# Differential attention: one combined pass over both halves, the first half's inverse applied when the output is stored, and a minimum of negated logits

## Chip, cores and metric

One core of a Trainium2 chip (trn2) runs the whole program, a chain of three transformer layers, in one launch. The metric is the device time of that launch in microseconds.

## The reference, cut to what matters

The changed stage is `diff_attention` of the second layer: 1024 tokens, 8 heads, query and key halves of 64, values of 128, in blocks of 128 queries.

```python
def diff_attention(q, k, v, lam, rel_table):
    ...
    def block(args):
        ...
        s = jnp.einsum("bqhcd,bkhcd->bhcqk", qi, k).astype(jnp.float32) * scale + bias[None, :, None]
        s = jnp.where(rel >= 0, s, -jnp.inf)
        p = jax.nn.softmax(s, axis=-1)
        w = p[:, :, 0] - lam * p[:, :, 1]
        return jnp.einsum("bhqk,bkhv->bqhv", w.astype(v.dtype), v)
```

Each head has two softmaxes, c = 0 and 1. With e the exponentials and z their sums, the weights are w = e0/z0 - lam e1/z1. The output of each head then goes through an RMS norm over its 128 values, a gain, and a gate.

## The kernel before

`diff_attend` (L2505) is one block of code on all engines, between barriers. The stages around it start after it and end before it. It walks through 8 heads, and in each through 8 blocks of 128 queries; block qb needs (qb + 1) x 128 keys, so every width from 128 to 1024 comes once a head. The first and the last head are written out, and the six between run in a hardware loop of two heads a turn. Every engine has its own fixed order of instructions, and semaphores connect them:

- TensorE, for each k: `logits` of block k + 2 (L2655; both halves, two matmuls for each 512 keys, into the one accumulator pS that a half has), `values` of block k - 1 (L2668, into one of two banks of pO), `turn` of block k (L2679, which transposes the weights W into pE). `logits` of block 0 of a head waits for GpSimd's split of that head's keys (`x_split`, L2657).
- VectorE, for each k: `bias` of block k + 1, `combine` of block k, `keep` of block k - 1; at k = 1 the `norm` of the head before, at k = 2 and 3 its `move_head`. `bias` (L2728) reads the logits from PSUM, adds the bias, scales, and keeps the row's maximum, for each half, and then negates both maxima (L2742). `combine` (L2744) takes the reciprocals of both sums (L2748), multiplies that of half 1 by the lambda factor (L2750; `lam` holds the negated factor), writes half 1 times it to W (L2753), and adds half 0 times its reciprocal (L2755). `keep` (L2758) copies the value product from PSUM to O (L2762).
- ScalarE, for each k: `exps` of block k + 1 (L2815: exponent with the negated maximum as bias, and the sum), `move` of block k (L2823, the transposed weights from PSUM to ET, L2827), `squares` of block k - 1 (L2829). At k = 1 comes the `root` of the head before (L2835), at k = 3 `round_head` of the next head (L2811, L2813).
- GpSimd, for each head: `gate` of the head before (L2620), `set_bias` of the next (L2601), `store`, and `subtract` of the next head (L2606), two long instructions at L2612 and L2615 that read and write SBUF and end with `x_split`.
- SyncE issues the loads of raw queries and keys and of values, a head ahead.

The lines that matter most:

```python
dve.tensor_scalar(v[:, :, 1:2], v[:, :, 0:1], -1.0, None, ALU.mult).then_inc(neg, 1)           # L2742
dve.tensor_scalar(W[:, qb % 2, 0:w], E[:, qb % 2, 1, 0:w], v[:, 1, 3:4], None, ALU.mult)        # L2753
dve.scalar_tensor_tensor(W[:, qb % 2, 0:w], E[:, qb % 2, 0, 0:w], v[:, 0, 3:4], W[:, qb % 2, 0:w],
                         ALU.mult, ALU.add).then_inc(comb, 1)                                   # L2755
dve.tensor_copy(O[:, s, qb, :], pO[:, qb % 2, 0:D_V]).then_inc(kept, 1)                         # L2762
```

Of the kernel before, what the change touches and what calls it, by code (L numbers as in the profile page):

```python
# [14 lines left out]
ACT = mybir.ActivationFunctionType  # L15
AX = mybir.AxisListType

P = 128
L = 1024
# [2485 lines left out]
def diff_attend(nc, tag, qkT, vg, skew, far, lam, subln, ident, yT):  # L2505
# [3 lines left out]
    with Place(nc, tag) as pl:  # L2509
# [9 lines left out]
        mx = pl.sb("mx", [P, 2, 2, 4])  # L2519
# [22 lines left out]
        neg = pl.sem("negated")  # L2542
        expd = pl.sem("exp_done")
        inv = pl.sem("weights_ready")
        half = pl.sem("second_half_weighted")
# [24 lines left out]
        with nc.Block() as block:  # L2570
# [150 lines left out]
            def _(dve):  # L2721
                dve.sem_inc(masked, 2)
                dve.sem_inc(comb, 2)
                dve.sem_inc(kept, 2)
# [3 lines left out]
                def bias(h, s, qb):  # L2728
                    w, m = (qb + 1) * P, h * TT + qb
                    v = mx[:, qb % 2, :, :]  # L2730
                    if qb == 0:
                        dve.wait_ge(b_in, h + 1)
                        dve.wait_ge(b_far, h + 1)
                    for a in range(2):
                        dve.wait_ge(dots, 2 * m + a + 1)
                        dve.wait_ge(expd, 2 * m + a + 1)
                        dve.sem_inc(passed, 1)
                        dve.tensor_tensor_reduce(S[:, qb % 2, a, 0:w], pS[:, a, :, :].rearrange("p a b -> p (a b)")[:, 0:w],  # L2738
                                                 B[:, s, L - w:L], D_QK ** -0.5, GONE, ALU.add, ALU.max,
                                                 v[:, a, 0:1]).then_inc(masked, 1)  # L2740
                    dve.wait_ge(masked, 2 * m + 4)
                    dve.tensor_scalar(v[:, :, 1:2], v[:, :, 0:1], -1.0, None, ALU.mult).then_inc(neg, 1)  # L2742

                def combine(h, qb):  # L2744
                    m, w = h * TT + qb, (qb + 1) * P
                    v = mx[:, qb % 2, :, :]
# [3 lines left out]
                    dve.tensor_scalar(v[:, 1, 3:4], v[:, 1, 3:4], lam[:, :], None, ALU.mult).then_inc(inv, 1)  # L2750
                    dve.wait_ge(inv, 2 * m + 2)
                    dve.wait_ge(turned, m + 1)
                    dve.tensor_scalar(W[:, qb % 2, 0:w], E[:, qb % 2, 1, 0:w], v[:, 1, 3:4], None, ALU.mult).then_inc(half, 1)  # L2753
                    dve.wait_ge(half, m + 1)
                    dve.scalar_tensor_tensor(W[:, qb % 2, 0:w], E[:, qb % 2, 0, 0:w], v[:, 0, 3:4], W[:, qb % 2, 0:w],  # L2755
                                             ALU.mult, ALU.add).then_inc(comb, 1)

                def keep(h, s, qb):  # L2758
                    dve.wait_ge(summed, h * TT + qb + 3)
                    if qb == 0:  # L2760
                        dve.wait_ge(h_tr, 2 * h + 2)
                    dve.tensor_copy(O[:, s, qb, :], pO[:, qb % 2, 0:D_V]).then_inc(kept, 1)  # L2762
# [19 lines left out]
                def body(h, s, r, first, last):  # L2782
                    if first:
                        bias(h, s, 0)
                    for k in range(TT):
# [5 lines left out]
                        if k > 0:  # L2791
                            keep(h, s, k - 1)
                        elif not first:
                            keep(h - 1, 1 - s, TT - 1)
# [5 lines left out]
                keep(D_H - 1, 1, TT - 1)  # L2800
# [5 lines left out]
            def _(act):  # L2806
                act.sem_inc(expd, 4)
                act.sem_inc(moved, 1)
                act.sem_inc(sqd, 2)

# [4 lines left out]
                def exps(h, qb):  # L2815
                    m, w = h * TT + qb, (qb + 1) * P
                    act.wait_ge(neg, m + 1)
                    act.wait_ge(comb, m + 1)
                    for a in range(2):
                        act.activation(E[:, qb % 2, a, 0:w], S[:, qb % 2, a, 0:w], ACT.Exp, bias=mx[:, qb % 2, a, 1:2],  # L2820
                                       accum_out=mx[:, qb % 2, a, 2:3]).then_inc(expd, 1)
# [17 lines left out]
                def body(h, s, r, first, last):  # L2839
# [3 lines left out]
                    for k in range(TT):  # L2843
# [5 lines left out]
                        if k > 0:  # L2849
                            squares(h, s, k - 1)  # L2850
                        elif not first:
                            squares(h - 1, 1 - s, TT - 1)
# [4 lines left out]
                heads(act, body)  # L2857
                squares(D_H - 1, 1, TT - 1)
# [623 lines left out]
```

## Time and profile before

| What | us |
| --- | --- |
| median of 3 runs | 4681.78 |
| lowest and highest of them | 4668.34, 4687.17 |
| profiled execution, its own time | 4683.71 |
| profiled execution, span from first to last instruction | 4682.1 |
| granted TensorE clock over the span, share of full speed | 0.904 |

The durations in this text come from that one profiled execution. TensorE is busy 87% of the span, VectorE 44%, ScalarE 33% and GpSimd 32%; these are means over many stages with different limits, and the changed stage lies from about 2812 to 3206 us.

In the views below an engine is PE (TensorE), PEld (its weight loads), DVE (VectorE), ACT (ScalarE) or POOL (GpSimd). L12 is line 12 of the kernel. Names before `<-` are what an instruction writes, behind it what it reads. `x64` is a count. A record in brackets is the idle time of the engine before the instruction, with the one that ended it. One matmul on 32-bit data leaves two records. The granted clock is given as a share of 2.4 GHz, so that 0.50 is 1.2 GHz.

### The profile page before, as it was taken

Reading aid. Unit: us, or ns where it says so; the run is one execution under the profiler, and the core shown is the slowest. Engines: PE = TensorE matmul, PEld = TensorE weight load, DVE = VectorE, ACT = ScalarE, POOL = GpSimd, SP = SyncE. Lnnn points to the kernel's source line nnn. Section 1 sums busy time; section 2 is a strip of 40 time slices with the busy share of each in tenths; the row PEclk is TensorE's granted clock in tenths of the full one; section 3 lists DMA queues with packets and bytes.
Section 4 is the critical chain, followed back from the end, with each engine's and each line's share of the span. In section 5 each row is a group of like instructions: output and inputs, shape, how many; then the busy total and the mean of one; then the engine's idle time right before and its main releaser. Section 6 shows DMA issues by size and latency. Waiting matters only on the chain. (4 is left out here: it accounts for less than half of the span.)

```text
span 4682.1 us, 54420 instructions
## 1 busy us (share of the span) xinstructions
PE 4070.8 (87%) x20836; PEld 3446.7 (74%) x20836; DVE 2053.7 (44%) x3708; ACT 1531.8 (33%) x2722; POOL 1506.9 (32%) x1157
## 2 busy tenths in 40 slices
PE   7799678689999899999997646667999999999878
PEld 6667566578888788788886535555889888889867
DVE  7479642323000024441110547773355656665523
ACT  2145323313000133211111325553345544554432
POOL 2322100033333144111110542323455555555433
PEclk9779767899999999989999767788999999999989
DMA  3222220353221343332221333224421111111044
GB/s 135 90 65 84 95 47 14 137 191 135 79 79 41 109 165 131 102 113 97 87 82 42 112 85 89 69 59 142 146 57 42 46 32 46 46 37 46 19 164 137
DMA packets 270719, 408.82 MB, mean 87 GB/s; under 512 B 42459, under 2 KB 171132, under 8 KB 269820
## 3 DMA queue, kind: packets, MB, share of 16 engines
q1 hardware_dynamic: 242684, 311.61, 21.7%
q0 software_dynamic: 25488, 89.73, 5.1%
q8 instruction: 157, 2.57, 0.2%
q10 hardware_dynamic: 2304, 4.20, 0.2%
q14 instruction: 86, 0.70, 0.1%
HBM read 293.46 MB, written 107.83 MB: 86 GB/s over the span
## 5 line engine op out<-in xcount | busy, mean ns | idle before, releaser
L115 PE MATMUL out_acc<-out_sw,out_sa 128*128 128x512 f32 x1920 | 446.8, 395 | 50.5 <-POOL out_sa L803 43.2
L115 PEld LDWEIGHTS out_acc<-out_sw,out_sa 128*128 128x128 f32 x1920 | 367.1, 191 | 130.2 <-issue 44.3
L115 PE MATMUL hg_acc<-l_XT,hg_ws 128*128 128x512 f32 x1440 | 360.9, 409 | 0.0
L115 PE MATMUL hg_acc<-l_first_ws,l_XT 128*128 128x256 f32 x2880 | 359.6, 284 | 0.0
L115 PEld LDWEIGHTS hg_acc<-l_first_ws,l_XT 128*128 128x128 f32 x2880 | 348.8, 192 | 0.0
L115 PEld LDWEIGHTS hg_acc<-l_XT,hg_ws 128*128 128x128 f32 x1440 | 279.1, 197 | 57.8
L3335 POOL TENSOR_TENSOR hg_DD<-hg_BB 128x256 f32<-128x256 f32 x224 | 155.8, 696 | 359.1 <-PE hg_pA L3099 232.6
L115 PE MATMUL up_acc<-ffn_XT,ffn_first_ws 128*128 128x512 f32 x1152 | 263.8, 391 | 2.6 <-PEq L55 2.6
L115 PE MATMUL down_acc<-down_sw,down_sa 128*128 128x512 f32 x1056 | 242.2, 392 | 19.7 <-POOL down_sa L803 17.3
L803 POOL TENSOR_TENSOR out_sa<-out_a,out_sa 128x512 fp32r<-128x512 f32 x80 | 174.9, 2186 | 255.8 <-ACT out_sw L702 255.8
L115 PEld LDWEIGHTS up_acc<-ffn_XT,ffn_first_ws 128*128 128x128 f32 x1152 | 217.3, 189 | 48.0 <-issue 2.7
L115 PEld LDWEIGHTS down_acc<-down_sw,down_sa 128*128 128x128 f32 x1056 | 199.4, 189 | 62.4 <-issue 18.0
L760 DVE TENSOR_TENSOR out_sw<-out_w,out_sw 128x1024 fp32r<-128x1024 f32 x80 | 106.5, 1334 | 303.6 <-ACT out_sw L702 303.6
L884 DVE TENSOR_TENSOR up_h<-up_acc,up_sil 128x512 f32<-128x512 f32 x44 | 30.4, 692 | 452.5 <-ACT up_sil L876 452.5
L115 PE MATMUL up_acc<-ffn_XT,up_ws 128*128 128x512 f32 x960 | 218.4, 389 | 0.0
L3193 DVE TENSOR_TENSOR hg_DD<-hg_Q,hg_DD 128x256 f32<-128x256 f32 x224 | 184.7, 825 | 75.8 <-ACT hg_DD L3264 75.7
L115 PEld LDWEIGHTS up_acc<-ffn_XT,up_ws 128*128 128x128 f32 x960 | 180.2, 188 | 37.4
L2664 PE MATMUL da_pS<-da_X 128*128 128x512 f32 (+3 forms) x384 | 111.3, 434 | 108.6 <-DVE da_mx L2738 73.0
L2073 ACT ACTIVATE even_stage<-even_acc 128x512 f32<-128x512 f32 (+1 forms) x88 | 49.3, 561 | 421.5 <-PE even_acc L115 421.4
L115 PE MATMUL am_g_acc<-l_XT,am_ws 128*128 128x512 f32 x768 | 179.1, 396 | 8.8 <-ACT am_stage L1308 8.8
L115 PE MATMUL even_acc<-l_XT,l_first_ws 128*128 128x512 f32 x768 | 177.9, 392 | 2.5 <-PEq L55 2.5
L2664 PEld LDWEIGHTS da_pS<-da_X 128*128 128x128 f32 x384 | 78.3, 241 | 136.8 <-DVE da_mx L2738 91.4
(489 smaller groups left out, 8441.8 us busy)
## 6 DMA issues: line engine op xcount, KB each, us to landing
l_first_raw<-in_odd_w_in SPq DMA_DIRECT2D x62, 512.0 KB, 5.4
down_w<-in_w_ffn_down SPq DMA_DIRECT2D x44, 512.0 KB, 4.0
da_raw<-q_k SPq DMA_DIRECT2D x32, 512.0 KB, 8.5
out_w<-in_even_w_out SPq DMA_DIRECT2D x32, 512.0 KB, 4.3
out_w<-in_odd_w_out SPq DMA_DIRECT2D x32, 512.0 KB, 4.1
even_w<-in_even_w_in SPq DMA_DIRECT2D x7, 2048.0 KB, 8.9
l_first_raw<-in_even_w_in SPq DMA_DIRECT2D x6, 2048.0 KB, 10.7
hidden<-up_h POOLq DMA_DIRECT2D x44, 256.0 KB, 2.3
```

The lines of the kernel that those rows point to most:

```text
L115: mm = pe.matmul(out, lhs(p, k), rhs(q, k), start=start and i == 0, stop=stop and i == n - 1)
L760: dve.tensor_tensor(sw[:, s, 1, :], w[:, i % 2, :], sw[:, s, 0, :].bitcast(F32), ALU.subtract).then_inc(w_split, 1)
L803: pool.tensor_tensor(sa[:, s, 1, :], a[:, i % 2, :], sa[:, s, 0, :].bitcast(F32), ALU.subtract).then_inc(a_split, 1)
L884: dve.tensor_tensor(h[:, i % 2, :], acc[:, i % 2, 1, :], sil[:, i % 2, :], ALU.mult).then_inc(gated, 1)
L2073: act.activation(stage[:, j % B, :n], acc[:, i % B, :n], func).then_inc(moved, 1)
L2664: mm = pe.matmul(pS[:, a, c // NC, 0:k], X[:, s, a, qb * P:(qb + 1) * P], X[:, s, 2 + 2 * part + a, c:c + k], start=part == 0, stop=part == 1)
L3193: last = dve.tensor_tensor(d, sides(x[:, s, :], h)[:, :, e, :, u, :], d, ALU.mult)
L3335: pool.tensor_tensor(factors(n, j, 1)[:, :, :, 1 - e, :], b[:, :, :, 1 - e, :], mid, ALU.subtract)
```

## The change

1. `bias` multiplies by the negated scale and takes the minimum, so that S holds negated logits and mx the negated maximum. L2742 and its semaphore go.
2. `exps` uses a scale of -1 and the minimum as its bias, and waits for each half's minimum by itself.
3. `combine` forms r = lam z0 / z1 in the [128 x 1] instruction L2750, and writes W = e0 + r e1 in one pass. L2753 and its semaphore go.
4. The missing factor 1/z0 is applied in `keep`, which moves from VectorE to ScalarE: a copy from PSUM with the reciprocal as its scale, in front of `squares`. For this mx has four slots instead of two.

```diff
-        mx = pl.sb("mx", [P, 2, 2, 4])
+        mx = pl.sb("mx", [P, 4, 2, 4])
...
                         dve.tensor_tensor_reduce(S[:, qb % 2, a, 0:w], pS[:, a, :, :].rearrange("p a b -> p (a b)")[:, 0:w],
-                                                 B[:, s, L - w:L], D_QK ** -0.5, GONE, ALU.add, ALU.max,
+                                                 B[:, s, L - w:L], -D_QK ** -0.5, -GONE, ALU.add, ALU.min,
                                                  v[:, a, 0:1]).then_inc(masked, 1)
-                    dve.wait_ge(masked, 2 * m + 4)
-                    dve.tensor_scalar(v[:, :, 1:2], v[:, :, 0:1], -1.0, None, ALU.mult).then_inc(neg, 1)
...
-                    dve.tensor_scalar(v[:, 1, 3:4], v[:, 1, 3:4], lam[:, :], None, ALU.mult).then_inc(inv, 1)
+                    dve.tensor_scalar(v[:, 1, 3:4], v[:, 1, 3:4], lam[:, :], v[:, 0, 2:3], ALU.mult, ALU.mult).then_inc(inv, 1)
                     dve.wait_ge(inv, 2 * m + 2)
                     dve.wait_ge(turned, m + 1)
-                    dve.tensor_scalar(W[:, qb % 2, 0:w], E[:, qb % 2, 1, 0:w], v[:, 1, 3:4], None, ALU.mult).then_inc(half, 1)
-                    dve.wait_ge(half, m + 1)
-                    dve.scalar_tensor_tensor(W[:, qb % 2, 0:w], E[:, qb % 2, 0, 0:w], v[:, 0, 3:4], W[:, qb % 2, 0:w],
+                    dve.scalar_tensor_tensor(W[:, qb % 2, 0:w], E[:, qb % 2, 1, 0:w], v[:, 1, 3:4], E[:, qb % 2, 0, 0:w],
                                              ALU.mult, ALU.add).then_inc(comb, 1)
-
-                def keep(h, s, qb):
-                    dve.wait_ge(summed, h * TT + qb + 3)
-                    if qb == 0:
-                        dve.wait_ge(h_tr, 2 * h + 2)
-                    dve.tensor_copy(O[:, s, qb, :], pO[:, qb % 2, 0:D_V]).then_inc(kept, 1)
...
+                def keep(h, s, qb):
+                    act.wait_ge(summed, h * TT + qb + 3)
+                    act.wait_ge(inv, 2 * (h * TT + qb) + 2)
+                    if qb == 0:
+                        act.wait_ge(h_tr, 2 * h + 2)
+                    act.activation(O[:, s, qb, :], pO[:, qb % 2, 0:D_V], ACT.Copy, scale=mx[:, qb % 4, 0, 3:4]).then_inc(kept, 1)
...
-                    act.wait_ge(neg, m + 1)
                     act.wait_ge(comb, m + 1)
                     for a in range(2):
-                        act.activation(E[:, qb % 2, a, 0:w], S[:, qb % 2, a, 0:w], ACT.Exp, bias=mx[:, qb % 2, a, 1:2],
-                                       accum_out=mx[:, qb % 2, a, 2:3]).then_inc(expd, 1)
+                        act.wait_ge(masked, 2 * m + a + 3)
+                        act.activation(E[:, qb % 2, a, 0:w], S[:, qb % 2, a, 0:w], ACT.Exp, scale=-1.0, bias=mx[:, qb % 4, a, 0:1],
+                                       accum_out=mx[:, qb % 4, a, 2:3]).then_inc(expd, 1)
...
                         if k > 0:
+                            keep(h, s, k - 1)
                             squares(h, s, k - 1)
                         elif not first:
+                            keep(h - 1, 1 - s, TT - 1)
                             squares(h - 1, 1 - s, TT - 1)
```

## Rows read from the trace of the kernel before

**Rows 1.** The head of the page.

```profile
span 4682.1 us, 54420 instructions
```

**Rows 2.** Busy time of the stage, by engine, with clock, DMA share and GB/s.

```profile
core 0: us, PE busy (x) PEld busy (x) DVE busy (x) ACT busy (x) POOL busy (x), PEclk, DMA share, GB/s
...
2812.00:3206.00 394.00, 253.83 (x1312) 214.09 (x1311) 300.92 (x680) 207.24 (x478) 95.46 (x44) 0.80 0.28 66
```

**Rows 3.** The waits in the stage: us in total, times, longest us.

```profile
PE da_pS L2664 <- DVE da_mx L2738: 73.0, 51, 5.3
PE da_pE L2686 <- DVE da_W L2755: 52.1, 24, 7.0
```

**Rows 4.** Groups by line, most by shape: count, busy us, mean ns, idle before.

```profile
L2753 DVE TENSOR_SCALAR da_W<-da_E,da_mx 128x128 f32<-128x128 f32 (+3 forms) x64 | 62.4, 975 | 2.4 <-DVE da_mx L2750 0.2
L2742 DVE TENSOR_SCALAR da_mx<-da_mx 128x2 f32<-128x2 f32 x64 | 36.3, 567 | 2.2
L2762 DVE COPY da_O<-da_pO 128x128 f32<-128x128 f32 x64 | 18.5, 289 | 40.2 <-PE da_pO L2675 40.1
...
L2753 DVE TENSOR_SCALAR da_W<-da_E,da_mx 128x768 f32<-128x768 f32 x8 | 33.0, 4123 | 0.3
L2753 DVE TENSOR_SCALAR da_W<-da_E,da_mx 128x896 f32<-128x896 f32 x8 | 5.5, 687 | 0.3
L2755 DVE SCALAR_TENSOR_TENSOR da_W<-da_E,da_mx,da_W 128x768 f32<-128x768 f32 x8 | 8.1, 1018 | 0.3
L2755 DVE SCALAR_TENSOR_TENSOR da_W<-da_E,da_mx,da_W 128x512 f32<-128x512 f32 x8 | 6.0, 751 | 0.3
L2738 DVE CUSTOM_DVE_ANT_0 da_S<-da_pS,da_B 128x1024 f32<-128x1024 f32 x16 | 18.9, 1218 | 0.0
L2827 ACT ACTIVATE da_ET<-da_pE 128x128 f32<-128x128 f32 x8 | 2.2, 278 | 12.7 <-PE da_pE L2686 12.7
L2827 ACT ACTIVATE da_ET<-da_pE 128x512 f32<-128x512 f32 x8 | 4.8, 597 | 9.8 <-PE da_pE L2686 9.8
...
L693 ACT ACTIVATE ffn_XT<-out_acc,out_gc 128x512 fp32r<-128x512 f32 x16 | 10.4, 686 | 1.7 <-PE out_acc L675 1.6
...
L1380 DVE CUSTOM_DVE_ANT_0 am_rel<-am_rel,am_score 128x1024 f32<-128x1024 f32 x1 | 1.2, 1226 | 0.0
```

**Rows 5.** One head in order of time: start us, us, engine, line.

```profile
3026.03 3.61 ACT L2813 ACTIVATE da_X<-da_raw 128x4096 fp32r<-128x4096 f32 x1
3029.83 4.57 POOL L2612 TENSOR_TENSOR da_X<-da_raw,da_X 64x2048 fp32r<-64x2048 f32 x1 [2.99 <-ACT da_X L2813]
...
3031.82 2.60 DVE L2742 TENSOR_SCALAR da_mx<-da_mx 128x2 f32<-128x2 f32 x1
...
3034.48 4.51 POOL L2615 TENSOR_TENSOR da_X<-da_raw,da_X 128x2048 fp32r<-128x2048 f32 x1
...
3034.77 4.63 DVE L2753 TENSOR_SCALAR da_W<-da_E,da_mx 128x768 f32<-128x768 f32 x1
...
3040.51 1.54 PE L2686 MATMUL da_pE<-ident,da_W 128*128 128x128 f32 x6 [6.36 <-DVE da_W L2755]
```

**Rows 6.** Another stage, in order of time: a like pass under GpSimd.

```profile
264.10 4.57 POOL L1403 TENSOR_TENSOR am_ws<-am_w,am_ws 128x2048 fp32r<-128x2048 f32 x1
264.40 4.81 DVE L1342 SCALAR_TENSOR_TENSOR am_score<-am_rel,att_wi,am_score 128x512 f32<-128x512 f32 x1
```

**Rows 7.** TensorE's long waits, in order of time: one of each kind.

```profile
2841.84 1.54 PE L2686 MATMUL da_pE<-ident,da_W 128*128 128x128 f32 x6 [6.99 <-DVE da_W L2755]
...
3014.04 2.82 PE L2664 MATMUL da_pS<-da_X 128*128 128x512 f32 x8 [4.39 <-DVE da_mx L2738]
3056.71 1.65 PE L2664 MATMUL da_pS<-da_X 128*128 128x384 f32 x4 [5.16 <-DVE da_mx L2738]
```

**Rows 8.** The clock after the first long wait, by stretch; columns as in rows 2.

```profile
2840.00:2845.00 5.00, 2.76 (x11) 2.31 (x12) 4.86 (x11) 1.58 (x4) 0.32 (x1) 0.50 0.56 113
...
2850.00:2855.00 5.00, 4.29 (x34) 3.98 (x34) 3.41 (x11) 3.27 (x13) 0.00 (x0) 1.00 0.47 97
```

More of the change, by code:

```diff
@@ L2541, in diff_attend @@
         masked = pl.sem("logits_biased")
-        neg = pl.sem("negated")
         expd = pl.sem("exp_done")
         inv = pl.sem("weights_ready")
-        half = pl.sem("second_half_weighted")
         comb = pl.sem("halves_combined")
@@ L2723, in _ @@
                 dve.sem_inc(comb, 2)
-                dve.sem_inc(kept, 2)
                 dve.sem_inc(h_mv, 1)
@@ L2729, in bias @@
                     w, m = (qb + 1) * P, h * TT + qb
-                    v = mx[:, qb % 2, :, :]
+                    v = mx[:, qb % 4, :, :]
                     if qb == 0:
@@ L2738, in bias @@
                         dve.tensor_tensor_reduce(S[:, qb % 2, a, 0:w], pS[:, a, :, :].rearrange("p a b -> p (a b)")[:, 0:w],
-                                                 B[:, s, L - w:L], D_QK ** -0.5, GONE, ALU.add, ALU.max,
+                                                 B[:, s, L - w:L], -D_QK ** -0.5, -GONE, ALU.add, ALU.min,
                                                  v[:, a, 0:1]).then_inc(masked, 1)
-                    dve.wait_ge(masked, 2 * m + 4)
-                    dve.tensor_scalar(v[:, :, 1:2], v[:, :, 0:1], -1.0, None, ALU.mult).then_inc(neg, 1)
                 def combine(h, qb):
                     m, w = h * TT + qb, (qb + 1) * P
-                    v = mx[:, qb % 2, :, :]
+                    v = mx[:, qb % 4, :, :]
                     dve.wait_ge(expd, 2 * m + 6)
@@ L2790, in body @@
                         combine(h, k)
[L2791 to L2794, printed above, removed]
                         if k == 1 and not first:
@@ L2799, in _ @@
                 heads(dve, body)
-                keep(D_H - 1, 1, TT - 1)
                 norm(D_H - 1, 1)
@@ L2809, in _ @@
                 act.sem_inc(sqd, 2)
+                act.sem_inc(kept, 2)
+                def keep(h, s, qb):
[4 more added lines that the diff above has]
+                    act.activation(O[:, s, qb, :], pO[:, qb % 2, 0:D_V], ACT.Copy, scale=mx[:, qb % 4, 0, 3:4]).then_inc(kept, 1)
                 def round_head(h, s):
@@ L2857, in _ @@
                 heads(act, body)
+                keep(D_H - 1, 1, TT - 1)
                 squares(D_H - 1, 1, TT - 1)
```

## The prediction

> **What bounds the kernel now.** I went from the page to the stage, then to its waits, and last to single instructions. The change touches only the differential-attention stage. That stage runs from 2812 to 3206 us of a span of 4682.1 us [rows 1]. The stretch row [rows 2] shows no engine full: in 394 us VectorE is busy 300.9, TensorE 253.8, ScalarE 207.2, and TensorE's granted clock averages 0.80. TensorE takes its work in a fixed order, and everything passes through it, so I keep the account there: 394 us are 254 us of work and 140 us of waits. The waits [rows 3] name VectorE: 73.0 us for the biased logits (L2738) and 52.1 us for the combined weights (L2755). The other 15 us are waits for ScalarE and the last head's end. VectorE itself stands 40.2 us at L2762, waiting for the value product [rows 4]. The bound is therefore a ring: VectorE is late, TensorE waits, and VectorE waits in its turn for TensorE's product.
>
> Why is VectorE late? Single instructions show it [rows 5]. ScalarE's rounding of the next head ends at 3029.64 (call this R); GpSimd then subtracts for 4.57 and 4.51 us. VectorE's negation L2742, of two elements a row, takes 2.60 us and ends as the first GpSimd instruction ends. L2753, 128x768, takes 4.63 us and ends as the second one does. Only then can L2755 run and TensorE transpose, after a wait of 6.36 us. TensorE has seven such waits, the first of 6.99 us and the others of about 6.4 (45.2 us in all). Another seven, of 4.39 us each, stand behind the head's norm (30.7 us), and two, of about 5.2 us, at the loop's turn (10.5 us) [rows 7]. That leaves 73.0 + 52.1 - 45.2 - 30.7 - 10.5 = 38.7 us of short waits.
>
> **What the change removes from VectorE.** L2753 goes: 62.4 us [rows 4]. Its 768 form averages 4.12 us where the wider 896 form takes 0.69; at 0.62 for itself, 8 x 3.50 = 28 us of this is blocking and 34.4 us work. L2742 goes: 36.3 us for 64, and at some 0.17 us each (10.9 us) the other 25.4 us is blocking. L2762 goes: 18.5 us of work and 40.2 us of waiting. Gross, that is 62.4 + 36.3 + 18.5 + 40.2 = 157 us, 40% of the stage. The question is how much comes back.
>
> **What it adds or moves, with no price of its own.** The logits' pass becomes a minimum of negated values. A minimum of the same kind at L1380 took 1226 ns for 128x1024 against 1218 for L2738 [rows 4]: nothing, within 0.01 us x 128 = 1 us either way. The extra multiply of the lambda factor by the first half's sum is in the same [128x1] instruction. The exponent takes a scale of -1 as a constant. The larger mx costs nothing. Between ends of 0 and 64 x 0.09 us for these I take 0; VectorE's slack covers them, and without that cover it would be up to 6 us. ScalarE may start on half 0 once that half's minimum is there, where it now waits for both and the negation: a gain of some 0.1 to 1.2 us a block, on an engine that mostly waits for TensorE, so taken as 0.
>
> **The copy that moves to ScalarE.** A 128x128 move from PSUM takes 0.28 us there (L2827). The scale from a tile adds about 0.09 us (0.685 against 0.597 for 128x512, L693 and L2827) [rows 4]. So 64 x 0.37 = 24 us are added to ScalarE's 207, which then has 231 us of work. Behind each copy now stand the square of the same block, the exponent of the next block but one, and on TensorE the value product that needs its bank. Its wait for the product is covered: it is queued behind the move L2827, whose transpose TensorE issues after that product. Ahead of the norm nothing covers it, so I charge 0.5 us a head, 7 x 0.5 = 3.5 us.
>
> **Where the blocking goes.** L2753 does not take its block away with it. The combined pass still reads two tiles in SBUF. No row of this stage shows such a pass under a long GpSimd instruction, but another stage does: L1342, the same operation, took 4.81 us for 128x512 while GpSimd subtracted for 4.57 us [rows 6], where L2755 is 0.75 us for that size. So I let L2755 be blocked. The Trainium skill, "SBUF — State Buffer", section "Who interferes with whom", says the same: a VectorE instruction with two SBUF inputs contends with a GpSimd instruction that reads SBUF, and the second to issue waits. By that rule the sum stands as below; were it not to hold here, the time would be rival 2's. It speaks against a part of the gain, and rows 6 agree with it.
>
> Walked from R: VectorE comes to L2742 of block 6 at R + 2.2 [rows 5], so the combined pass of block 5 could start a few tenths later, and is held until the first subtraction ends at R + 4.8. It ends at R + 5.8 with 1.02 us of its own (768) [rows 4]. Its first consumer, the transpose, then waits some 1.5 us instead of 6.4. But the second subtraction, itself held by this pass, ends at about R + 10.2, and TensorE's next item is the next head's first logits, which need it. That wait, hidden today, becomes some 3.5 us. **Late next is GpSimd's subtraction.** The seven long waits go from 45.2 to 7 x (1.5 + 3.5) = 35 us: **-10 us**, with bounds 0 and -20 (if the passes slip in earlier).
>
> **The short waits.** Per block VectorE's path loses 34.4/64 = 0.54 us (L2753), 0.17 (L2742), 0.29 (L2762) and 0.63 (its wait): 1.63 us, against a mean short wait of TensorE of 38.7/64 = 0.60 us. Most therefore goes. What stays is turnaround at narrow blocks, where TensorE and VectorE hand two accumulators to and fro. I take 10 us as staying: **-28 us**, bounds -14 and -38.7. The norm's waits stay and get **+3.5**; the two at the loop's turn stay. Together -10 - 28 + 3.5 = **-35 us**.
>
> **The clock.** After the long wait the granted clock is 0.50 from 2840 to 2850 (1.2 GHz) and 1.00 (2.4 GHz) after it [rows 8]. Seven such spells of 10 us, with some 8.5 us of work that would take half, are worth 7 x 4.2 = 29 us at most, and 0 at least if the 3.5 us wait lowers the clock as well. VectorE and ScalarE also set the pace there, so I take **-8**.
>
> **Sum.** -35 - 8 = -43 us against the profiled execution's own 4683.7 us: 4640.7. That execution was 1.9 us above the median of the three runs, 4681.8; against the median it is 4639 us. The stage would take some 351 us instead of 394. The stages around it are closed off and stay.
>
> **Rivals.**
> (1) *The chain rounding, subtraction, logits sets each head's pace* and ScalarE, now with more in front of each rounding, starts it hardly sooner. For it: after R nearly nothing but the 10 us above is gained. Against it: from one long wait's end to the next rounding VectorE is busy almost throughout. The short waits then give only 14 and the clock nothing: 10 + 14 - 3.5 = 20 us, 4661. Chance 0.13.
> (2) *The combined pass is not held*, because its own second read finds a gap. Rows 6 speak against it. The first wait of 1.5 us goes, and the subtraction ends 1 us sooner: another 7 x (1.5 + 1) = 17 us, 4622. Chance 0.06.
> (3) *The clock follows*: with no wait over 4 us but the norm's, the spells of 0.50 after the subtraction vanish, and short waits vanish wholly. 10 + 38.7 - 3.5 + 20 = 65 us, 4617. Chance 0.12.
> (4) *The clock falls instead and stays at 0.50 through the stage*, as its waits become shorter but as many. TensorE's 254 us at 0.80 are then 406 us. Even if all short waits vanish, 35 us at the norm and 10.5 at the loop's turn stay: 452 us against 394, so 4740, slower. It decides below a mean clock of c where 254 x 0.80/c + 103 = 394, that is 0.70. Against it: the 0.50 spells follow the long waits, and these get shorter. Chance 0.03.
> (5) *The change does not do what it says*: a minimum that needs a second pass over the logits. L1380's row speaks against it. At 1.2 us for each of the sixteen 1024 forms, and the other widths in proportion (4.5 times the columns in all), it would add 16 x 1.2 x 4.5 = 86 us of VectorE. Chance 0.01.
>
> **How the numbers follow.** Forecast 0.65 (its own range 4625 to 4655), rivals 0.13, 0.06, 0.12, 0.03 and 0.01. The range runs from rival 3's 4617 less the rest of its clock term, 4612, to just past rival 1, 4663, and leaves out some 0.15. A change below 0.5%, 23 us or 4658, is about what a measurement of this kernel can tell from none. Rival 1 falls mostly within it, with a little of the forecast's upper end: same 0.12. Slower is rivals 4 and 5, 0.04. Faster 0.84.
>
> **What would show it.** Right: 64 passes at L2755's place where 128 were, no L2742; one 768 pass a head of about 3.5 us and one 896 pass of 2 to 3 us; the TensorE wait for the combined weights under 20 us; a new wait for GpSimd at the first logits of a head of some 25 us; ScalarE busy some 24 us more; a stage of 340 to 365 us. The walk is wrong if no pass is longer than its uncontended time, or if TensorE's wait of 6.4 us stands. The sum is wrong if the short waits stay near 38 us with VectorE idle beside them, or if the stage's clock leaves 0.78 to 0.90.

## The result, and the profile after

| What | before | after |
| --- | --- | --- |
| median of five runs each, side by side, us | 4681.78 | 4637.65 |
| lowest and highest of them | 4668.34, 4687.17 | 4624.20, 4645.26 |
| profiled execution, its own time | 4683.71 | 4645.26 |
| its span | 4682.1 | 4643.6 |
| the changed stage, first logits to last store | 393.8 | 353.0 |

The ratio of after to before is 0.9906, with a 95% interval of 0.9882 to 0.9931: faster by 0.94%, 44 us in the medians. The forecast was 4639 us. In the profiled executions the spans differ by 38.5 us. The stage is 40.8 us shorter. It starts 4.2 us later (2815.8 instead of 2811.6), and what lies behind it is 1.9 us shorter.

The head of the page, which answers to [rows 1]:

```profile
span 4643.6 us, 54306 instructions
```

The stage by engine, with the columns of [rows 2]:

```profile
core 0: us, PE busy (x) PEld busy (x) DVE busy (x) ACT busy (x) POOL busy (x), PEclk, DMA share, GB/s
2816.00:3169.50 353.50, 236.14 (x1312) 203.78 (x1312) 222.13 (x488) 227.12 (x543) 101.16 (x44) 0.81 0.30 73
```

VectorE has 79 us less work (300.9 before), ScalarE 20 more (207.2), and TensorE 18 less (253.8), though its instructions are the same. ScalarE now has more work than VectorE, and still nothing is full.

TensorE's waits in the stage, which answer to [rows 3] (us in total, times, longest):

```profile
PE da_pS L2662 <- POOLq L2616: 59.4, 8, 35.3
PE da_pS L2662 <- DVE da_mx L2735: 54.7, 23, 5.6
PE da_pO L2673 <- ACT da_ET L2817: 16.2, 24, 2.2
PE da_pE L2684 <- DVE da_W L2748: 13.3, 7, 2.8
```

The wait for the combined weights fell from 52.1 to 13.3 us. A new one has come, for GpSimd's split of keys. Its 59.4 us hold 35.3 of the time ahead of the stage's first logits; the other 24.1 us are seven waits of 2.9 to 3.7. The wait for the logits fell from 73.0 to 54.7.

The groups by line, which answer to [rows 4]:

```profile
L2748 DVE SCALAR_TENSOR_TENSOR da_W<-da_E,da_mx 128x128 f32<-128x128 f32 (+3 forms) x64 | 83.0, 1298 | 2.8
L2799 ACT ACTIVATE da_O<-da_pO,da_mx 128x128 f32<-128x128 f32 x64 | 23.0, 359 | 1.4 <-PE da_pO L2673 1.4
L2748 DVE SCALAR_TENSOR_TENSOR da_W<-da_E,da_mx 128x768 f32<-128x768 f32 x8 | 24.3, 3036 | 0.3
L2748 DVE SCALAR_TENSOR_TENSOR da_W<-da_E,da_mx 128x896 f32<-128x896 f32 x8 | 19.5, 2440 | 0.3
L2748 DVE SCALAR_TENSOR_TENSOR da_W<-da_E,da_mx 128x1024 f32<-128x1024 f32 x8 | 10.3, 1285 | 0.8
```

One pass a block is left. The 1024 form takes 1.29 us, the narrower 768 and 896 forms 3.04 and 2.44: these two stand under GpSimd's subtractions. The 384 form is held as well, 1.15 us where L2755 took 0.63 before: it starts under GpSimd's gate (L2620, 2.37 us). The moved copy costs 0.36 us.

One head in order of time, beside [rows 5]:

```profile
2962.19 3.61 ACT L2803 ACTIVATE da_X<-da_raw 128x4096 fp32r<-128x4096 f32 x1
2965.99 4.55 POOL L2610 TENSOR_TENSOR da_X<-da_raw,da_X 64x2048 fp32r<-64x2048 f32 x1 [3.40 <-ACT da_X L2803]
2968.18 3.17 DVE L2748 SCALAR_TENSOR_TENSOR da_W<-da_E,da_mx 128x768 f32<-128x768 f32 x1
2970.61 5.12 POOL L2613 TENSOR_TENSOR da_X<-da_raw,da_X 128x2048 fp32r<-128x2048 f32 x1
2971.41 0.88 PE L2684 MATMUL da_pE<-ident,da_W 128*128 128x128 f32 x6 [1.75 <-DVE da_W L2748]
2974.06 2.62 DVE L2748 SCALAR_TENSOR_TENSOR da_W<-da_E,da_mx 128x896 f32<-128x896 f32 x1
2975.93 1.11 PE L2662 MATMUL da_pS<-da_X 128*128 128x128 f32 x4 [3.65 <-POOLq L2616]
2992.76 0.20 DVE L2755 RECIPROCAL da_hs<-da_hs 128x8 f32<-128x8 f32 x1 [3.50 <-ACT da_hs L2827]
2994.89 2.82 PE L2662 MATMUL da_pS<-da_X 128*128 128x512 f32 x8 [5.48 <-DVE da_mx L2735]
```

Here R, the end of the rounding, is 2965.80. The 768 pass ends at R + 5.55 (walked: R + 5.8), the second subtraction at R + 9.93 (10.2), TensorE waits 1.75 us for the weights (1.5) and 3.65 for the split (3.5). The walk from R holds to some 0.3 us. The last two rows are the norm's wait, 5.5 us where it was 4.39 [rows 7].

**The account.** TensorE's stage, before and after, in us, by the terms of the prediction:

| Term | before | after | change | predicted |
| --- | --- | --- | --- | --- |
| seven waits for weights, and the new ones for the split | 45.2 | 13.3 + 24.1 | -7.8 | -10 |
| seven waits behind the norm | 30.7 | 38.6 | +7.9 | +3.5 |
| two waits at the loop's turn | 10.5 | 0 | -10.5 | 0 |
| short waits | 38.7 | 54.7 - 38.6 = 16.1 | -22.6 | -28 |
| waits of L2673 for ScalarE's move | 6.1 | 16.2 | +10.1 | 0 |
| TensorE's own work | 254.2 | 236.3 | -17.9 | -8 |
| stage | 393.8 | 353.0 | -40.8 | -43 |

What is missing from the sums, 8.4 us, is the same before and after (7.2 of it are the waits at the last head's end).

The total came out within some 2 us of the forecast, though five of the six terms did not: the terms miss by +2, +4, -10.5, +5, +10 and -10 us, and the misses cancel.

### The profile page after: what moved, and what is told of

Same layout as the page of the kernel before. It is cut to its first block and busy times, and to the rows that moved or that the text cites. A ratio compares the mean times of both kernels' runs of the same rounds, so it can differ in the third digit from the quotient of the medians.

```text
span 4643.6 us, 54306 instructions
## 1 busy us (share of the span) xinstructions
PE 4055.8 (87%) x20836; PEld 3440.2 (74%) x20836; DVE 1975.3 (43%) x3516; ACT 1550.2 (33%) x2786; POOL 1513.1 (33%) x1157
## 5 line engine op out<-in xcount | busy, mean ns | idle before, releaser
L2662 PE MATMUL da_pS<-da_X 128*128 128x512 f32 (+3 forms) x384 | 108.3, 429 | 114.2 <-POOLq L2616 59.4
L115 PEld LDWEIGHTS up_acc<-ffn_XT,up_ws 128*128 128x128 f32 x960 | 180.2, 188 | 37.4
L701 ACT ACTIVATE out_sa<-out_a 128x512 fp32r<-128x512 f32 x80 | 50.5, 631 | 385.7 <-DMA out_w<-in_w_out 141.7
```

The source lines that it names most:

```text
L115: mm = pe.matmul(out, lhs(p, k), rhs(q, k), start=start and i == 0, stop=stop and i == n - 1)
L701: act.activation(sa[:, s, 0, :], a[:, i % 2, :], ACT.Copy)
L2662: mm = pe.matmul(pS[:, a, c // NC, 0:k], X[:, s, a, qb * P:(qb + 1) * P], X[:, s, 2 + 2 * part + a, c:c + k], start=part == 0, stop=part == 1)
```

## The experiments

Each kernel is the changed kernel with one edit, unless said. "Stage" is measured from the first logits to the issue of the last store, in one profiled execution of each kernel. The first three take back one part each.

The arguments below rest on the stage and its waits, and not on small differences of the program's time. The code outside the stage is the same in all fourteen kernels, and yet it took 4273 to 4294 us in their profiled executions, and the runs of one kernel lie up to 30 us apart. No kernel was profiled twice; two pairs that differ by an edit of almost no effect (the changed kernel and `round_earlier`, `mean_earlier` and `both_earlier`) agree in the stage within 0.7 us.

**The negation back.** Maximum, then VectorE negates, and the exponents wait for it.

```diff
-  B[...], -D_QK ** -0.5, -GONE, ALU.add, ALU.min, v[:, a, 0:1]).then_inc(masked, 1)
+  B[...], D_QK ** -0.5, GONE, ALU.add, ALU.max, v[:, a, 0:1]).then_inc(masked, 1)
+ dve.tensor_scalar(v[:, :, 1:2], v[:, :, 0:1], -1.0, None, ALU.mult).then_inc(neg, 1)
...
- act.activation(E[...], S[...], ACT.Exp, scale=-1.0, bias=mx[:, qb % 4, a, 0:1], ...)
+ act.activation(E[...], S[...], ACT.Exp, bias=mx[:, qb % 4, a, 1:2], ...)
```

> The changed kernel with the maximum and VectorE's negation L2742 back, everything else as changed. Stage of the changed kernel: 353.5 us from the first logits to the last store; of before: 394. Theory A (the block moves): the negation returns to the place behind block 6's logits pass, is held by GpSimd's first subtraction (some 2.5 us), and the combined pass of block 5 behind it is then held by the second one (some 5 us in all). TensorE's seven waits for W go back from 1.75 to about 6.4 us, its waits of 3.6 us for the subtraction vanish: stage 365 to 375 us. Theory B (work alone counts): 64 x 0.17 = 11 us of VectorE beside its slack: stage 353 to 358 us. Theory C (code loading at the loop's turn): two stalls of 5 us come back only if VectorE's loop body is again too long; 32 instructions more a turn may or may not do it.

Measured: 4650.78 us (eight runs), ratio to before 0.9929, interval 0.9907 to 0.9951, which overlaps that of the changed kernel; stage 363.8 us. Six of the seven waits for the weights are back at 6.33 us, and those for the split are gone. The first head kept its 1.7 for the weights and 2.9 for the split. One head:

```profile
2965.74 4.55 POOL L2611 TENSOR_TENSOR da_X<-da_raw,da_X 64x2048 fp32r<-64x2048 f32 x1 [3.40 <-ACT da_X L2806]
2966.40 3.92 DVE L2740 TENSOR_SCALAR da_mx<-da_mx 128x2 f32<-128x2 f32 x1
2970.37 4.50 POOL L2614 TENSOR_TENSOR da_X<-da_raw,da_X 128x2048 fp32r<-128x2048 f32 x1
2970.73 4.96 DVE L2751 SCALAR_TENSOR_TENSOR da_W<-da_E,da_mx 128x768 f32<-128x768 f32 x1
2975.74 1.54 PE L2685 MATMUL da_pE<-ident,da_W 128*128 128x128 f32 x6 [6.33 <-DVE da_W L2751]
```

The negation, two elements a row, is held by the first subtraction, and ends as it ends. The combined pass comes up just behind the start of the second one, and is held by that for its whole length.

**The two passes back.** Half 1 times r to W, then half 0 added.

```diff
- dve.scalar_tensor_tensor(W, E[..1..], v[:, 1, 3:4], E[..0..], ALU.mult, ALU.add)
+ dve.tensor_scalar(W, E[..1..], v[:, 1, 3:4], None, ALU.mult).then_inc(half, 1)
+ dve.wait_ge(half, m + 1)
+ dve.scalar_tensor_tensor(W, E[..0..], 1.0, W, ALU.mult, ALU.add)
```

> The changed kernel with two combining passes, W = r E1 and then W = E0 + W, everything else as changed. Theory A: the tensor_scalar pass of block 5 is held by the first subtraction, runs 0.6 us, and the second pass of block 5 is held by the second subtraction: TensorE's wait for W is back at 6 us or more, plus 34 us of VectorE's work of which a part is in its slack. Stage 370 to 385 us. Theory B (work alone): 34 us on VectorE's path, no change in TensorE's longest waits: stage 375 to 388 with the waits spread over all blocks. Rival: VectorE has 120 us of idle time now, so it is hidden: stage under 362 us.

Measured: 4654.75 us (six runs), ratio 0.9939, interval 0.9919 to 0.9960; stage 370.0 us, waits for the weights 6.5 us each, none for the split. The same picture with other names:

```profile
2957.14 4.57 POOL L2611 TENSOR_TENSOR da_X<-da_raw,da_X 64x2048 fp32r<-64x2048 f32 x1 [3.40 <-ACT da_X L2806]
2959.34 2.79 DVE L2749 TENSOR_SCALAR da_W<-da_E,da_mx 128x768 f32<-128x768 f32 x1
2961.79 4.69 POOL L2614 TENSOR_TENSOR da_X<-da_raw,da_X 128x2048 fp32r<-128x2048 f32 x1
2962.17 5.13 DVE L2751 SCALAR_TENSOR_TENSOR da_W<-da_E,da_W 128x768 f32<-128x768 f32 x1
```

So it takes **both** removals: with either instruction left in front, the combining pass arrives under the second subtraction.

**The copy back on VectorE**, with the inverse as its factor.

```diff
- act.activation(O[...], pO[...], ACT.Copy, scale=mx[:, qb % 4, 0, 3:4]).then_inc(kept, 1)
+ dve.tensor_scalar(O[...], pO[...], mx[:, qb % 4, 0, 3:4], None, ALU.mult).then_inc(kept, 1)
```

> The changed kernel with the output's copy (scaled by the first half's inverse) on VectorE again instead of ScalarE. Theory A: VectorE gets back 64 x 0.29 us and its waits for the value product (40 us before); the blocking stays as changed (combined passes of 3.0 and 2.4 us for widths 768 and 896), the norm's wait falls by some 0.5 to 1 us a head. Stage 358 to 366 us. Rival: the move to ScalarE was the main gain, since VectorE stood 40 us for the product: stage over 372 us. Rival 2: it was worth nothing or less, as ScalarE's 24 us lie in front of the norm: stage 345 to 355 us.

Measured: 4643.4 us (four runs), ratio 0.9905, interval 0.9877 to 0.9933; stage 356.1 us, between the ranges of theory A and rival 2. The move to ScalarE is thus worth only 3.1 us of the stage, and no difference in the time that the runs can tell. TensorE's account shows why. With the copy on ScalarE the short waits are 18.0 us lower (34.1 to 16.1) and TensorE's work 5.1. But the norm's waits are 7.9 us higher (7 x 4.39 to 38.6), those for ScalarE's move 9.8 (6.4 to 16.2) and those for weights and split together 2.3. The sum is -3.1.

**Negation and copy both back**, so that only the combined pass is left of the change. The edit is the first and the third diff above together.

> The changed kernel with both the negation and the output's copy on VectorE again, and only the single combined pass left of the change. VectorE's loop body has 301 instructions, against 317 before and 267 and 269 with one of the two. Theory A (no joint effect): stage 353 + 10 + 3 = 366 us, of which the waits for W are 6.3 us and those at the norm 4.4 us, and no wait at the loop's turn. Theory C (the loop's turn depends on where the waiting for the product stands behind a late VectorE): the two waits of 5 us come back, stage 375 to 385 us.

Measured: 4663.14 us (one run), stage 388.0 us. Apart, the two parts cost 10.8 and 3.1 us; together they cost 35.0. The waits for the weights are 5.7 us each (the first 6.2), the norm's 4.39, VectorE waits 65.9 us for the value product, and the pause at the loop's turn has partly returned (3.1 us in TensorE's waits, twice). The stage is above the range of theory C (375 to 385). The combined pass alone saves only 393.8 - 388.0 = 5.8 us, with a copy on VectorE that now scales as well (0.35 us instead of 0.29).

**No subtraction.** Both subtractions work on 8 columns. In the other columns the kernel leaves out the split: the low parts of the keys are zero, and those of the queries stay what ScalarE wrote there, the rounded queries, which then count twice in the logits. (The expectation takes both as zero.) So this kernel does not compute the logits of the reference any more; its other instructions and their shapes are the same, and only its times are read here.

```diff
- pool.tensor_tensor(X[D_QK:P, s, 0:2, :], raw[D_QK:P, 0:2, :], X[D_QK:P, s, 0:2, :].bitcast(F32), ALU.subtract)
+ pool.tensor_tensor(X[D_QK:P, s, 0:2, 0:8], raw[D_QK:P, 0:2, 0:8], X[D_QK:P, s, 0:2, 0:8].bitcast(F32), ALU.subtract)
...
- pool.tensor_tensor(X[:, s, 4:6, :], raw[:, 2:4, :], X[:, s, 2:4, :].bitcast(F32), ALU.subtract)
+ pool.tensor_tensor(X[:, s, 4:6, 0:8], raw[:, 2:4, 0:8], X[:, s, 2:4, 0:8].bitcast(F32), ALU.subtract)
...
+ pool.memset(X[:, :, 4:6, :].bitcast(F32), 0.0)
```

> The changed kernel with GpSimd's two subtractions cut to 8 columns each; the low parts of queries and keys are otherwise left out (zero), so the logits are those of the rounded values. Theory A: both the lock on VectorE's passes and TensorE's wait for the subtraction vanish, that is 7 x (1.75 + 3.5) = 37 us, less what the next engine, ScalarE after its rounding, then sets: combined passes of 768 and 896 at 1.02 and 1.15 us; stage 318 to 335 us. Rival (rounding on ScalarE, 3.6 us a head with 7.4 us of exponents and moves behind it, is the real bound): stage 342 to 352 us, with the same gap at the same place named for ScalarE or VectorE.

Measured: 4588.81 us (one run), stage 306.5 us, mean clock 0.87. Inside the stage TensorE waits neither for weights nor for the split. The groups by shape:

```profile
L2751 DVE SCALAR_TENSOR_TENSOR da_W<-da_E,da_mx 128x896 f32<-128x896 f32 x8 | 9.2, 1152 | 0.3
L2751 DVE SCALAR_TENSOR_TENSOR da_W<-da_E,da_mx 128x768 f32<-128x768 f32 x8 | 8.2, 1019 | 0.3
```

The same passes that took 2.44 and 3.04 us take 1.15 and 1.02: the hold is GpSimd's. The stage gained 46.5 us, more than any theory gave: 37.4 of waits for weights and split and 17.0 of TensorE's work, with 7.4 given back in other waits.

**The subtractions in quarters**, four instructions of 256 columns each.

```diff
- pool.tensor_tensor(X[:, s, 4:6, :], raw[:, 2:4, :], X[:, s, 2:4, :].bitcast(F32), ALU.subtract)
+ for i in range(4):
+     q = slice(i * (L // 4), (i + 1) * (L // 4))
+     pool.tensor_tensor(X[:, s, 4:6, q], raw[:, 2:4, q], X[:, s, 2:4, q].bitcast(F32), ALU.subtract)
```

> The changed kernel with each of GpSimd's two subtractions in four instructions of 256 columns. Theory A: a combined pass now waits for the end of a quarter (1.15 us) and not of the whole: the 768 and 896 passes take about 1.5 to 2.2 us instead of 3.0 and 2.4, TensorE's wait of 1.75 us for W falls under 0.5 us; the wait for the subtraction stays at 3 to 4 us, since the same work ends it and each pass that slips in delays it by its own length. Stage 345 to 352 us. Rival: a waiting pass gets in only when GpSimd has nothing queued, so that it waits for all four quarters: passes as long as now or longer, stage 353 to 365 us.

Measured: 4649.3 us (one run), stage 365.0 us. The pass does slip in, as theory A says, and the time is at the end of the rival's range.

```profile
2965.12 5.71 POOL L2612 TENSOR_TENSOR da_X<-da_raw,da_X 64x512 fp32r<-64x512 f32 x4 [3.40 <-ACT da_X L2807]
2967.31 1.15 DVE L2752 SCALAR_TENSOR_TENSOR da_W<-da_E,da_mx 128x768 f32<-128x768 f32 x1
2970.90 5.78 POOL L2617 TENSOR_TENSOR da_X<-da_raw,da_X 128x512 fp32r<-128x512 f32 x4
2976.87 1.11 PE L2666 MATMUL da_pS<-da_X 128*128 128x128 f32 x4 [7.43 <-POOLq L2620]
```

The wait for the weights is gone. But four quarters take 5.7 us where the whole took 4.55. One by one, three of them take 1.26 to 1.29 us, and the third, which starts at 2967.60 under VectorE's pass, 1.99: the cut costs some 0.4 us, and the pass that slips in some 0.7. TensorE's next logits start 11.9 us after the rounding instead of 10.1, and TensorE, earlier by the wait it no longer has, stands 7.4 us for them (theory A said 3 to 4). The late item is the subtraction's end, not the pass.

**The rounding a block earlier** (at k = 2 instead of 3), so that the subtraction may start earlier.

```diff
-                        if k == 3 and not last:
+                        if k == 2 and not last:
                             round_head(h + 1, 1 - s)
```

> The changed kernel with ScalarE's rounding of the next head after block 2 instead of block 3, so that GpSimd's subtraction starts one block (about 5 us) sooner. Theory A (the subtraction is late for the next head's logits): TensorE's seven waits of 3.6 us for the subtraction vanish; the held passes are then those of widths 640 and 768, and its wait of 1.75 us for W stays. Stage 353 - 25 = 328, give or take 8 us. Rival (the whole 46 us of the subtraction is the lock on VectorE's passes): the lock falls on other blocks and the stage stays at 348 to 356 us.

Measured: 4639.48 us (four runs), ratio 0.9889, interval 0.9862 to 0.9915; stage 352.4 us, the waits for the split still 3.64. This missed. GpSimd's rows say why:

```profile
2965.85 0.59 POOL L2624 DMA_DIRECT2D y_even<-da_YT  x1 [8.77 <-DVE da_YT L2766]
2969.14 4.58 POOL L2610 TENSOR_TENSOR da_X<-da_raw,da_X 64x2048 fp32r<-64x2048 f32 x1 [2.69 <-DMA y_even<-da_YT]
```

GpSimd's order has `store` of the head before in front of `subtract`. The rounding of this head ended at 2963.86, and the subtraction started 5.3 us later. Of these, 2.0 went by until VectorE had the head before ready to store, 0.6 in issuing the store, and 2.7 until its DMA had landed: all for a transfer that the subtraction has no use for.

**The mean and root a block earlier** (mean at k = 0 and normalization at k = 1 on VectorE, root at k = 0 on ScalarE).

```diff
 # VectorE
+                        if k == 0 and not first:
+                            mean(h - 1, 1 - s)
                         if k == 1 and not first:
                             norm(h - 1, 1 - s)
 # ScalarE
-                        if k == 1 and not first:
+                        if k == 0 and not first:
                             root(h - 1, 1 - s)
```

> The changed kernel with the norm's mean on VectorE and its root on ScalarE one block sooner (k = 0), and the rest of the norm where it is. Theory A (TensorE's seven waits of 5.5 us stand behind VectorE's wait of 3.5 us for the root, which is two table loads, a copy and squares on ScalarE): those waits fall to 2 us or less, new ones of 1 us may stand at the mean. Stage 353 - 20 = 333, give or take 8 us. Rival (ScalarE's table loads are themselves on the chain, wherever they stand): stage 348 to 356 us, with the wait moved to block 0.

Measured: 4613.26 us (four runs), ratio 0.9844, interval 0.9816 to 0.9872; stage 329.1 us, as theory A says. The waits behind the norm fell from 5.5 to 2.0 us.

**Both of these together**, the last two diffs in one kernel.

> Both at once. If the two waits are independent parts of the chain, their gains add: stage about 308 us, 300 to 320, the program 40 to 45 us below the changed kernel, near 4595 us. Rival: with both gone, ScalarE (227 us of work and its waits for the transposes) or the clock sets the pace and the sum of the two gains isn't reached: stage 320 to 335 us.

Measured: 4614.5 us (five runs), ratio 0.9844, interval 0.9822 to 0.9865; stage 328.7 us. The stage is in the rival's range, but not for its reason: the earlier rounding adds nothing here either, since the subtraction again stands for the store, 2.69 us of it for the DMA. In the head from 2948.76 on the rounding ends at 2952.37 and the subtraction starts at 2956.46, 4.1 us later.

**The store behind the subtraction**, on top of both.

```diff
-                    if not first:
-                        store(h - 1)
                     if not last:
                         subtract(h + 1, 1 - s)
+                    if not first:
+                        store(h - 1)
```

> Both earlier moves (rounding a block earlier, mean and root a block earlier), and in GpSimd's order the store of the head before now stands behind the subtraction instead of in front of it. My theory: the earlier rounding gained nothing because the first subtraction then stood 2.7 us behind the store's completion in GpSimd's queue (row of both_earlier: 2.69 us, ended by the DMA of y_even). If so, the subtraction starts some 2.7 us sooner a head, and the wait of TensorE for it at a head's first logits (3.65 us in both_earlier) falls to about 1 us: 7 x 2.7 = 19 us, a stage of 308 to 314 us against 328.7, and a time of 4592 to 4600 us. Rival: something else holds the chain. The passes of VectorE then simply meet the subtraction at other blocks, and are held by it as before: the wait stays above 3 us and the stage within 325 to 332 us. A third outcome is possible: the wait for the subtraction goes, and the held passes show up as a longer wait for the combined weights, for a gain of 5 to 12 us.

Measured: 4597.47 us (four runs, 4596.53 to 4598.24), ratio 0.9827, interval 0.9794 to 0.9861; stage 308.4 us. Waits, and one head:

```profile
PE da_pS L2662 <- DVE da_mx L2735: 47.8, 49, 2.1
PE da_pS L2662 <- POOLq L2616: 35.7, 1, 35.7
PE da_pE L2684 <- DVE da_W L2748: 16.9, 13, 1.8
```

```profile
2940.74 4.57 POOL L2610 TENSOR_TENSOR da_X<-da_raw,da_X 64x2048 fp32r<-64x2048 f32 x1 [6.57 <-ACT da_X L2808]
2942.87 3.12 DVE L2748 SCALAR_TENSOR_TENSOR da_W<-da_E,da_mx 128x640 f32<-128x640 f32 x1
2945.39 5.05 POOL L2613 TENSOR_TENSOR da_X<-da_raw,da_X 128x2048 fp32r<-128x2048 f32 x1
2948.44 2.81 DVE L2748 SCALAR_TENSOR_TENSOR da_W<-da_E,da_mx 128x768 f32<-128x768 f32 x1
```

The subtraction now starts 0.2 us after the rounding. Only the stage's first wait for the split is left of eight; the others are gone, where about 1 us each was expected: the store had cost 4.1 us and not only the 2.7 of its DMA. Apart from one wait of 4.7 us for ScalarE in the first head, no wait of TensorE between the stage's first logits and its last head's end is over 2.1 us. The holds are still there, now on the 640 and 768 passes. The granted clock of the stage is 0.89, and TensorE's work 220.0 us. Against both_earlier's 328.7 us: -21.9 for the split (6 x 3.65), -9.6 of work, +7.0 and +3.9 of short waits for logits and weights. This version beats both kernels; the last three edits together are worth 44.6 us of the stage (40 us of the program's time), about as much as the change itself (40.8 and 44).

**Padding.** Does the pause at the loop's turn depend on the length of VectorE's loop body? Eight increments of a semaphore that nobody waits for were added to each `combine`, and in a second kernel eighteen.

```diff
                     dve.wait_ge(inv, 2 * m + 2)
+                    for _ in range(8):
+                        dve.sem_inc(pad, 1)
                     dve.wait_ge(turned, m + 1)
```

> The changed kernel with eight semaphore increments that nobody waits for in each of VectorE's combine steps, 128 instructions more in a turn of the loop. In the changed kernel VectorE has no stall of 5 us at the loop's turn, and the queue of 8 KB instruction loads that is busy at the turns before (18 loads in the stage) does nothing between 2935 and 3125 us. Theory (code loading): with the padding the loop body is too long again, the loads come back at each turn, and with them two VectorE waits of about 5 us with the releaser 'issue': stage 353.5 + 10 to 18 us. Rival: the stalls before came from VectorE being late, not from the number of instructions: no wait of 5 us, the stage within 353 to 358 us.

> The changed kernel with eighteen semaphore increments in each combine step. VectorE's loop body then has 509 instructions; it has 317 in the kernel before, 235 in the changed one and 349 with eight increments, where no stall came back. Theory (length alone, with a limit above 349): the loads of 8 KB return at each turn and two VectorE waits of about 5 us with them. Rival (length is not the cause): no such wait at any length. Each increment costs VectorE about 0.1 us (from the run with eight), so 10 x 0.1 us x 64 = 64 us more of VectorE than there, of which a part is in slack: stage 385 to 425 us without the stalls.

Measured: with eight, 4650.91 us (one run), stage 360.1, no pause at the turn: the theory missed, and the stage is 2 us above its rival's range. With eighteen, 4657.84 us (one run), stage 381.1, and the pause is back, in a stage shorter than was expected without it. VectorE's waits there, the increments themselves and the pauses:

```profile
DVE da_W L2751 <- issue: 116.1, 64, 2.1
DVE da_S L2736 <- issue: 15.6, 2, 7.8
```

The bodies, counted in VectorE's instruction list, are 317 long before, 235 after, 349 and 509 with the paddings, and 301 with negation and copy back. The pauses are 5.3 us at 317, none at 235 and 349, 7.8 at 509 and 3.2 at 301. The count alone does not order the cases. The bodies of 235 and 509 differ in the increments only, but these make VectorE later too, by 1.8 us a block; so it is not shown whether the length or the lateness brings the pause. Where a limit lies stays open.

## Why the prediction was right

**Where the blocking goes** was the step that decided, and it is shown. The pass is held with the subtraction and not without it (3.04 against 1.02 us for 768 columns), and the walk from R fits each of its four times to some 0.3 us. The Trainium skill, "SBUF — State Buffer", section "Who interferes with whom", gives the rule by which it was walked; these runs agree. Rival 2, a pass that is not held, is refuted: its 4622 us lie below all five runs (4624.20 the lowest), and the passes of 3.04 and 2.44 us contradict it. What the prediction did not say is that half of this change would have left the 6.4 us wait as it was: two things stood in series in front of the weights, one for each subtraction, and the two restorations show that either is enough to catch the second hold (the negation in six heads of seven).

**Late next is GpSimd's subtraction**: right in place and size, 24.1 us where 7 x 3.5 = 24.5 was said. The sum of both waits fell by 7.8 (said: 10). Rival 1, the chain from rounding to the logits, was refuted as a forecast of 4661, but this chain is one of two that limit the kernel after: with the subtraction sooner (store_behind, against both_earlier) or gone (no_subtraction) the stage falls by 20 and 46 us. The other is the norm's: mean_earlier takes 24 us.

**The short waits** fell by 22.6 us (said: 28), inside the bounds of 14 to 38.7. What stays was put in the wrong place. It is not turnaround at narrow blocks: of the 16.1 us left, 15.5 are seven waits of 0.94 and seven of 1.28 us, in front of the logits of the 768 and 896 blocks:

```profile
2957.71 1.71 PE L2662 MATMUL da_pS<-da_X 128*128 128x512 f32 x8 [0.94 <-DVE da_mx L2735]
2962.24 1.97 PE L2662 MATMUL da_pS<-da_X 128*128 128x512 f32 x8 [1.28 <-DVE da_mx L2735]
```

At both places VectorE first moves the head before (`move_head`, 0.75 us, at 2956.16 and 2960.56) and then reads the logits that TensorE waits to overwrite. Waits of 0.94 to 1.28 us stood at these places before, too. Nearly all the other short waits are gone.

**The copy that moves to ScalarE** was priced rightly for itself (23.0 us, said: 24) and wrongly in what stands behind it. "Its wait for the product is covered", and 3.5 us for the norm: the norm's waits grew by 7.9, and TensorE's wait for the move L2817, set at nothing, by 10.1. With the copy back on VectorE both are as before (4.39 us each, and 6.4 in all, where before had 6.1), so the copy is the cause. In front of the root, ScalarE now has two exponents, a move, a copy and a square, and TensorE comes to its wait sooner. The step missed what the moved copy delays: ScalarE's next move, and with it TensorE.

**The two at the loop's turn stay**: wrong, by 10.5 us. The trace of before had the hint. VectorE stands there for "issue", which no other engine releases:

```profile
2954.28 0.42 DVE L2738 CUSTOM_DVE_ANT_0 da_S<-da_pS,da_B 128x256 f32<-128x256 f32 x1 [5.37 <-issue]
```

```profile
q14 instruction: 2, 0.02, 0.7%
```

The second row, of the DMA queues in the trace of before from 2950 to 2957 us, shows two loads of instructions, one inside that pause (2948.91 to 2954.28) and one just behind its end. A third, between 2949 and 2950, lies inside it as well. Each of the six pauses, in before, with the long padding and with negation and copy back, has three such loads, one or two of them inside it and the rest within some us behind. From 110 us behind the stage's start to 45 us before its end that queue has 12 loads in before, none in after, 15 with the long padding, 12 with negation and copy back, and 2 or fewer in each of the ten other kernels. Many loads go with the pauses in every one of them. That the load is what VectorE waits for is not shown.

**The clock**: said -8, between 0 and -29. TensorE's work fell by 17.9 us. By stretches of 1 us, with those between the two levels counted in proportion, its work at a granted 0.50 (1.2 GHz) fell from 116.7 to 96.4 us; at twice the speed half of that is saved, 10.1 us, against the 8 that were said. The other 7.8 us are not explained by the clock. Work times clock, that is the same matmuls at full speed, should be equal in all kernels, and comes out as 196 us before, 188 after, 194 in keep_on_vector, 190 in both_earlier and 195 in store_behind: matmul ends are modelled, and a scatter of this size is in the row of the account. Rival 3 (the spells of 0.50 vanish) did not come in this kernel. In store_behind, where nearly no wait is over 2.1 us, the clock rose to 0.89 and the work at 0.50 fell to 51 us, which is what rival 3 described. Rival 4, a clock that falls, is refuted: 0.81 where 0.80 was. Rival 5 too: the 1024 form of the minimum, L2735, takes 1213 ns where the maximum took 1218 [rows 4].

Two small slips in the working change nothing: rival 3's 4617 less the rest of its clock term (29 - 20 = 9) is 4608 and not 4612, and the 103 us in rival 4's threshold have no source (140 - 35 = 105 give the same 0.70).

So the forecast of 4639 us met 4637.65 with its decisive step right, and with errors of 4 to 10 us in five other terms that largely cancelled. That it met the median within 2 us is luck: the five runs spread over 21 us, and the two profiled spans differ by 38.5 us and not by 44. The range of 4612 to 4663 was no wider than such errors ask for.

## What to carry to other kernels

Where an engine's small instruction ends exactly as a long instruction of another engine ends, count how many such instructions stand in series in front of the consumer: each can catch a hold of its own, and removing one of two gains little (5.8 us here for the largest part alone, 40.8 for all). When a wait is removed, ask which fixed queue the next late item stands in, and what it has in front of it there: a store that waits for its data and for its own DMA held the subtraction for some 4 us a head, and moving it behind was worth 20 us. Work moved to an engine with time to spare is not free if that engine's next instruction feeds the bound: 18 us of short waits were saved and 18 us came back elsewhere.

## What the runs showed of the hardware

- A VectorE instruction of two elements a row in SBUF (L2740) took 3.92 us under GpSimd's subtraction and 0.17 without. In after, L2745, of one element a row, took 0.27 us at each of its 64 places, under a subtraction too.
- The second subtraction takes 5.12 us when a pass of VectorE runs at its start and 4.50 when not, so the hold works both ways.
- Cut in four, a GpSimd subtraction of 2048 columns took 5.71 us instead of 4.55. A piece takes 1.27 us (median of 32) where a quarter of 4.55 is 1.14, and one that starts under a pass of VectorE 1.99.
- VectorE paused for 5.3 us at the turn of a loop of 317 instructions and 7.8 us at one of 509, with loads of 8 KB each on the instruction queue (12 loads, 0.10 MB). The Trainium skill, "Advanced Engine Details and Errata", section "ISA Cache", gives an instruction cache of 32 KB in lines of 16 KB for engines other than TensorE. It counts 256 instructions to a line; two lines then hold 512, an estimate from that page, and every body here has fewer. By this figure alone none should have to be loaded again, and the runs differ: 317 and 301 had pauses and loads, 349 had not, and the loads are 8 KB. The measurement decides, and it does not say what the limit is.
